# ScalarE evicts each chunk before it converts the next weights, in the layer groups and the MLP

## The reference

```
h = rms_norm(x) * (1 + sc_m) + sh_m
proj = h @ w_in                                  # 1024 x 12296, split into 11 parts
y_ret = silu(rg) * head_norm(retention(rope(rq), rope(rk), rv))
y_lru = gelu(ly) * rg_lru(causal_conv(lx))
y_fox = forgetting_attention(fq, fk, fv, log_sigmoid(ff))
merged = g0 * (y_ret @ ret_w_o) + g1 * (y_lru @ lru_w_o) + g2 * (y_fox @ fox_w_o)
x = x + gt_m * rms_norm(merged @ w_out)
h = rms_norm(x) * (1 + sc_f) + sh_f
x = x + gt_f * rms_norm(square(relu(h @ w1)) @ w2)   # hidden width 4096
```

## Time and profile before

| | |
|---|---|
| median of three runs | 2360.78 us |
| the profiled execution's own time | 2359.27 us |
| its span, first to last instruction | 2357.7 us |
| mean granted TensorE clock | 0.90 |
| TensorE busy | 1994.4 us (85%) |
| VectorE busy | 1392.8 us (59%) |
| ScalarE busy | 772.2 us (33%) |
| GpSimd busy | 650.2 us (28%), nearly all in the first 700 us |
| instructions | 34501 |

### The profile page before, as it was taken

The page is one execution under the profiler, slowest core; times in us unless marked ns, Lnnn a source line. Parts: engine busy times, 40 slices in busy tenths (PEclk is TensorE's granted clock), DMA queues, the critical chain, the costliest instruction groups (busy, mean ns, idle before and its releaser), DMA issues.

```text
span 2357.7 us, 34501 instructions
## 1 busy us (share of the span) xinstructions
PE 1994.4 (85%) x14362; PEld 1882.6 (80%) x14362; DVE 1392.8 (59%) x1452; ACT 772.2 (33%) x854; POOL 650.2 (28%) x392
## 2 busy tenths in 40 slices
PE   6295369688579999999998869999899989789997
PEld 3295349587568989799998867999699989787997
DVE  0878775666847884544466665454535465755453
ACT  1221200000022333342546533444334436533442
POOL 7999999999891000000000000000000000000000
PEclk9596677878788998899999989999999999989999
DMA  9353333333353444353444342454244444432552
GB/s 403 122 195 136 136 113 110 118 114 108 108 199 113 161 151 158 112 184 119 144 160 151 139 157 90 165 193 162 90 160 144 145 142 161 143 121 93 179 179 90
DMA packets 51935, 345.94 MB, mean 147 GB/s; under 512 B 6112, under 2 KB 8160, under 8 KB 12128
## 3 DMA queue, kind: packets, MB, share of 16 engines
q1 hardware_dynamic: 35712, 258.63, 30.9%
q0 software_dynamic: 13888, 81.80, 10.0%
q10 hardware_dynamic: 2208, 3.60, 0.4%
HBM read 334.57 MB, written 9.44 MB: 146 GB/s over the span
## 4 chain that ended last, share of the span: by engine, by line
PE 66%; DVE 24%; ACT 5%; issue 4%; DMA 1%; DVEq 0%; ACTq 0%; SPq 0%
PE ps L362 16%; PE ps L364 16%; PE ps L363 16%; DVE w_lo L1228 4%; ACT w_hi L870 3%; PE ps L440 2%; PE ps L575 2%; PE ps L563 2%; PE ps L573 2%; DVE gacc L1578 2%; DVE y_kv L1346 2%; PE ps L458 1%; DVE act_lo L1261 1%; PE ps L469 1%; DVE rstd L1248 1%
## 5 line engine op out<-in xcount | busy, mean ns | idle before, releaser
L362 PE MATMUL ps<-act_hi,w_hi 128*128 128x256 f32 x2672 | 780.5, 292 | 137.1 <-DVE act_lo L1261 103.5
L1228 DVE TENSOR_TENSOR w_lo<-raw,w_hi 128x2048 fp32r<-128x2048 f32 x211 | 510.7, 2421 | 638.0 <-ACT w_hi L870 637.6
L363 PE MATMUL ps<-act_lo,w_hi 128*128 128x256 f32 x2672 | 770.0, 288 | 0.0
L364 PE MATMUL ps<-act_hi,w_lo 128*128 128x256 f32 x2672 | 769.4, 288 | 0.0
L870 ACT ACTIVATE w_hi<-raw 128x2048 fp32r<-128x2048 f32 (+1 forms) x233 | 428.7, 1840 | 672.2 <-PE ps L364 668.9
L362 PEld LDWEIGHTS ps<-act_hi,w_hi 128*128 128x128 f32 x2672 | 528.1, 198 | 144.5 <-issue 57.2
L363 PEld LDWEIGHTS ps<-act_lo,w_hi 128*128 128x128 f32 x2672 | 528.3, 198 | 0.8
L364 PEld LDWEIGHTS ps<-act_hi,w_lo 128*128 128x128 f32 x2672 | 527.2, 197 | 0.0
L316 POOL TENSOR_TENSOR ada_raw<-ada_raw,silu_c 128x2048 f32<-128x2048 f32 x64 | 235.5, 3680 | 9.3 <-DMA ada_raw<-ada 8.4
L317 POOL TENSOR_TENSOR ada_raw<-ada_raw 128x1024 f32<-128x1024 f32 x64 | 173.4, 2710 | 5.0
L362 PE MATMUL ps<-mlp_hi,w_hi 128*128 128x256 f32 x512 | 144.4, 282 | 3.6 <-DVE mlp_lo L1854 3.6
(11 more groups left out here) (374 smaller groups left out, 3199.1 us busy)
## 6 DMA issues: line engine op xcount, KB each, us to landing
raw<-stream SPq DMA_DIRECT2D x233, 1024.0 KB, 4.8
ada_raw<-ada POOLq DMA_DIRECT2D x64, 1024.0 KB, 5.5
ada_part<-ada_acc POOLq DMA_DIRECT2D x64, 128.0 KB, 2.1
ada_f<-ada SPq DMA_DIRECT2D x4, 1024.0 KB, 17.9
ada_in<-ada_part POOLq DMA_DIRECT2D x2, 2048.0 KB, 9.8
ada_a<-ada SPq DMA_DIRECT2D x3, 1024.0 KB, 27.5
ada_in<-ada_part ACTq DMA_DIRECT2D x1, 2048.0 KB, 8.7
ada_in<-ada_part POOLq DMA_DIRECT2D x2, 1024.0 KB, 6.3
```

What stands on the lines that cost most here:

```text
L362: mm(out, ah, bh, start=first, stop=False)
L363: mm(out, ah, bl, start=False, stop=False)
L364: return mm(out, al, bh, start=False, stop=last)
L1228: tt(w_lo[:, s2, :], raw[:, s4, :], w_hi[:, s2, :].bitcast(f32), ALU.subtract).then_inc(S("lo_ready"), 1)
```

## The change

In `job` and `group` of ScalarE the eviction of chunk n is written ahead of the conversion for chunk n+2. The MLP hook is cut in two: on ScalarE the relu eviction comes ahead of the conversion and `mlp_hi` behind it; on VectorE the square comes ahead of the low part of the weights and `mlp_lo` behind it. No instruction is added or removed, and the other hooks keep their place behind both. The loops of the up and down projections, of Q and KV, and the LRU chunk are as before.

```diff
@@ ScalarE, job @@
                         n = n0 + c + 2
+                        if hook:
+                            hook[0](i, c)
+                        else:
+                            evict(dst(i + c), (j0 + c) % 2, i + (n0 + c), func, scale, ps[:, (j0 + c) % 2, sl])
                         if isinstance(i, int):
                             prep(i + n, (i + n) % RAW, (i + n) % 2)
                         else:
                             prep((i + n, i * (16 // RAW) + (n // RAW * 16 + 16)), n % RAW, n % 2)
                         if hook:
-                            hook(i, c)
-                        else:
-                            evict(dst(i + c), (j0 + c) % 2, i + (n0 + c), func, scale, ps[:, (j0 + c) % 2, sl])
+                            hook[1](i, c)
@@ ScalarE, group @@
                         n = n0 + off + c
+                        evict(dst(c), (j0 + JL(off) + c) % 2, n)
                         prep(n + 2, (n + 2) % RAW, n % 2)
-                        evict(dst(c), (j0 + JL(off) + c) % 2, n)
@@ ScalarE, MLP @@
-                    def mlp_steps(i, c, n=n, j=j, hf=hf):
+                    def mlp_relu(i, c, n=n, j=j):
+                        s = (j + c) % 2
+                        evict(relu[:, s, :], s, i + (n + c), ACT.Relu)
+
+                    def mlp_split(i, c, j=j, hf=hf):
                         s = (j + c) % 2
                         e = 8 * (2 * L + hf) + i + c
-                        evict(relu[:, s, :], s, i + (n + c), ACT.Relu)
                         act.wait_ge(S("mlp_sq"), e + 1)
...
-                    job(n, j, 8, None, hook=mlp_steps)
+                    job(n, j, 8, None, hook=(mlp_relu, mlp_split))
@@ VectorE, MLP @@
-                    def mlp_steps(i, c, j=j, hf=hf):
+                    def mlp_square(i, c, j=j):
+                        s = (j + c) % 2
+                        dve.wait_ge(S("evicted"), i + (j + c + 1))
+                        tt(rsq[:, s, :], relu[:, s, :], relu[:, s, :], ALU.mult).then_inc(S("mlp_sq"), 1)
+
+                    def mlp_low(i, c, j=j, hf=hf):
...
-                    job(n, 8, hook=mlp_steps)
+                    job(n, 8, hook=(mlp_square, mlp_low))
```

More of the change, by code:

```diff
@@ L1845, in _ @@
                     j = j0 + JL(L_MLP) + 16 * hf
-                    def mlp_steps(i, c, j=j, hf=hf):
+                    def mlp_square(i, c, j=j):
[3 more added lines that the diff above has]
+                    def mlp_low(i, c, j=j, hf=hf):
                         s = (j + c) % 2
                         e = 8 * (2 * L + hf) + i + c
-                        dve.wait_ge(S("evicted"), i + (j + c + 1))
-                        tt(rsq[:, s, :], relu[:, s, :], relu[:, s, :], ALU.mult).then_inc(S("mlp_sq"), 1)
                         dve.wait_ge(S("mlp_hi"), e + 1)
```

## The result

| | before | after |
|---|---|---|
| median of 6 runs each, same chip | 2360.99 us | 2371.9 us (2367.13 to 2375.41) |
| ratio, 95% interval | | 1.0044 [1.0031, 1.0057] |
| profiled execution | 2359.27 us | 2367.13 us |
| its span | 2357.7 us | 2365.6 us |

The change makes the kernel slower, by 0.3 to 0.6%. The profiled pair differs by 7.86 us; the prediction's sum was 8.53. The total came out close, but several terms inside it did not, and that is what the rest is about.

A forecast was written before the change was run, and what follows sets the result against it. TensorE was taken as the limit most of the time, otherwise waiting behind VectorE and ScalarE. 9.24 + 0.81 + 0.86 - 2.38 = 8.53 us on 2359.27 gave 2367.8, plus 1.51 for the median 2369.3; range 2362.5 to 2373.5 us.

The forecast's parts named there:

- The price of one step: The 512-column eviction now ahead of `w_hi` delays it by 0.48 us, with bounds of 0.47 and 0.57.
- FOXO, entry and scores: In each layer, FOXO's first matmul (waiting for `act_lo`) and the scores (behind the rope sum) each start 0.48 us later.
- LRUO and WOUT: At the entries to LRUO and WOUT, `w_hi` is on the chain; 0.48 us longer each, per layer.
- LRU: At the entry to LRU, `w_hi` is on the chain; 0.48 us longer per layer.
- G0 to RETO: From G0 until RETO0, two conversions lie on the chain; 0.96 us longer per layer.
- G1: At G1, two conversions lie on the chain until the transposes; 0.96 us longer per layer.
- Softplus and G1's low part: Two low parts of weights without full slack come late: 0.25 us at softplus and 0.15 at G1, per layer.
- y_sum: Sum of the MLP's halves, behind a chunk down's `w_hi` and `w_lo`: 0.27 us later at three places, 0.81 in all.
- The MLP: Last chunk up of layer 1's two halves: TensorE's wait for `mlp_lo` gets 1.19 us shorter each, 2.38 in all.
- absorbed: Rival: at most of the nine places the later `w_hi` is caught up before TensorE needs it; 2363.9 us, chance 0.17.
- Faster by the clock: Rival: shifted stalls remove lower-clock stretches at RETO, LRUO, WOUT and LRU, 2.2 us each; 2350 us, chance 0.06.
- Dearer: Rival: fox and RG chunks are late too, and `w_lo` eats the MLP's gain; 2373.5 us, chance 0.10.

The follow-up runs named there:

- nine steps alone: The kernel before, with eviction first only at LX2, FOXO0, LY3, G1_0, G1_1, G0_1, G0_2, RETO2 and LRUO3 of each layer; 2375.55 us, ratio 1.0055.

## Why the prediction was right, and where its terms were not

The forecast (slower, on the waits of `w_hi`) held, and so did the mechanism: the evictions added to the chain made the stalls behind it longer. The measured 2371.9 us is 2.6 above the predicted 2369.3 and inside the range. That the sum is so near is in part luck, as the terms show. One of the prediction's own signs of being wrong did come, too: the clock's rows differ at the same stalls. Against the traces, by the prediction's own steps:

- *The price of one step*, 0.48: a little too high. The stalls at LRU, LRUO and WOUT grew by 0.42 us. The 0.47 from start to start was read rightly, but before the change the conversion began 0.09 us behind TensorE's end and after it 0.51 (1282.52 to 1282.61, 1284.18 to 1284.69), so 0.42 is added. From the mark of FOXO0 to the scores it is 0.49, of which 0.06 is the mark's own shift.
- *Plain chunks cost nothing*: right, 5.76 us in all traces.
- *FOXO, entry and scores*, 0.48 each: there, 0.42 each in every trace (0.36 to 0.49 by the marks). The entry was bound with no stall to see; after the change it has one of 0.35 us.
- *LRUO and WOUT*, 0.48 each: the stall grew as said, but the time did not. The means of old and new differ by 0.1. This is 1.9 of the 8.5 us. The step that failed is the sum itself, which took a longer stall to be a later end of the chunk behind it.
- *LRU*, 0.48: 0.45 in the mean, but with a scatter of 0.8 us in the old order and 1.1 in the new, and in the pair itself it got 0.05 longer in layer 0 and 0.23 shorter in layer 1. In three of the eight new ones (over 21.3 us) the low stretch lasted 10.2 us, in all the others 6.8.
- *G0 to RETO*, 0.96: from the end of G0_0 to RETO0's first matmul it grew by the full 0.96 in layer 0 of the pair (24.08 to 25.04 us), but to RETO0's end only by 0.71, and by 0.51 in layer 1.
- *G1*, 0.96: 0.75 to 0.97 where the clock held, 2.4 to 2.6 in four of the six new ones. The term was sized at 1.9 for both layers; in the profiled pair it was 4.9. The prediction had seen a 1.64 us stretch behind a 1.8 us stall and put it in the range, but weighed it only where stalls got shorter, not where one of 2.1 grew to 2.6.
- *Softplus and G1's low part*, 0.40 together: softplus nothing. G1_1 did get late, 6.00 us instead of 5.76 (forecast 0.15), in each trace in which RG has the new order, but beside the chain: with G1 as before the stall ahead of the transposes is shorter by as much (1.72 us against 1.97 in layer 1 of before), and the end does not move.
- *The norm behind WOUT*, -0.1: nothing gained. Its stall did shrink, 3.63 to 3.43 us, but the next one grew from 1.17 to 1.39 in layer 0; between TensorE's ends the stretch is 0.00 and 0.12 longer.
- *y_sum*: between TensorE's ends, 0.19 us from layer 0 to layer 1, forecast 0.27, and nothing at the other two places (5.74 us in both), so 0.19 and not 0.81 in all.
- *The first block*, 0.86: the last chunk of OUT1 ends 0.8 us later in the pair (703.1 and 703.9), but the traces scatter by 6 us there, with no order by variant, so it stays open.
- *The MLP*, -1.19 twice: right, both stalls are 1.15 us shorter. In this pair the slow chunk down went too (39.72 to 38.08 us), the 1.64 kept out of the sum.

What the list leaves out is chance. In the pair two chunks outside the places that the sum prices took longer, at a longer or an added low stretch: the first chunk of G2 in layer 1 from 14.13 to 15.78 us, and the first chunk down of the second half of layer 0 from 9.09 to 10.64. In the other ten traces both come and go with either order (12.6 to 15.8, and 9.1 to 12.4). Together with the slow chunk down that went, they added 1.6 us to the pair.

So errors of about 3 us on either side cancelled: G1 dearer by the clock; LRU, LRUO, WOUT and part of RETO cheaper by the clock, with 1.6 us of chance on top. The first two are one fact: the cost of an added stall depends on which level the clock is at behind it. Of the rivals, "absorbed" had a true core (two of the nine places, in each layer), for another reason than it gave. "Faster by the clock" is out: the first chunks behind long stalls got 0.4 us cheaper, not 2.2. "Dearer" is out: nine steps alone are as slow as all, and the MLP's gain came in full.

At LRUO the lower level ended nearly as long after RETO3 as before, 13.6 us in before and 13.4 in after (layer 0), although TensorE resumed 0.42 later. Part of the cover follows from that: at the lower level TensorE works at about half its pace (11 matmuls in a window of 2 us instead of 19), so a resumption 0.42 us later costs about 0.21 if the low stretch ends at the same moment. Measured was about 0.1 in the mean. The Trainium skill says in "TensorE: Matmul & The Clock Gate", section "Part 1: The HAM clock gate", that the gate's beat is free-running. The varying slow stretches behind equal stalls agree with it (at G1 in the new order, four of six). The steady swallowing at LRUO and WOUT does not follow from it by itself: by our reasoning a beat with no relation to the program would give the full 0.42 in the mean. Why it is so steady stays open.

## What to carry to other kernels

When an engine evicts and also prepares the next operand, look at what waits for each before choosing the order: here nobody waited for the bank, and the chain ran through the conversion at nine places a layer, while in the MLP it ran through the eviction. Price an added stall by the clock behind it as well: fill stalls of 2 us and more with matmuls that nobody reads before moving half microseconds around, since that alone gave 8 us of 2360. And put marks at equal places in both traces, the untouched stretches too: a total that fits can be two wrong terms and some chance.

## What the runs showed of the hardware that was not expected

- A stall of TensorE of 1.8 to 2.9 us can be followed by 1.5 to 1.6 us of loss at the lower clock level: at G1 behind four of six stalls of 2.6 to 2.9 us and one of eight of 1.7 to 2.1; at WOUT0 with 1.87 us left, in all four; at LRU and LRUO0 with 2.0 us left, in two of four, and with 1.6 left in none of twelve. With 0.65 us at the head of the first chunk down of layer 1, never.
- After stalls of 8.7 and 9.3 us (WOUT0, LRUO0) the chunk behind loses about 2 us at the lower level, and with a stall longer by 0.42 it loses about 0.3 less of it in the mean.
- Filling four stalls and a part of G1's wait with matmuls of 512 columns took 1.9 to 2.5 us from each of LRU, RETO0 and LRUO0 and raised the mean granted clock of the profiled execution from 0.90 to 0.914.
- Chunks down of the same work take 5.44 us each in some halves and 5.65 in others, in runs of five or more, at a granted clock of 1.00 and with either order: up to 1.5 us in a half. What sets it is open.
